# RWKV-7 mixer stage: two inverse streams interleaved at another distance, and other work moved around them

## The reference, cut to what matters

```python
hn = _rms_norm(h, e_norm_mix)
p = hn @ e_w_in                                   # 1024 -> 512 + 512 + 1792
pu, pv, pb = _split(p, [A_WIDTH, A_WIDTH, B_IN])
ya = _chunked_sgu(jax.nn.gelu(pu), jax.nn.gelu(pv), sgu_ln_g, sgu_ln_b, sgu_w, sgu_b)
yb = _rwkv7_time_mix(pb, ...)
h = h + jnp.concatenate([ya, yb], axis=-1) @ e_w_out
...
def _rwkv7_scan(r, w, k, v, kk, a):               # 8 heads of 64, one step a token
    def step(S, inp):
        r_t, w_t, k_t, v_t, kk_t, a_t = inp
        sa = jnp.einsum('bhij,bhj->bhi', S, kk_t)
        ...
```

## Time and profile before

| what | value |
|---|---|
| median of three runs | 1999.3 us (1998.69 to 2001.7) |
| the profiled execution's own time | 1999.16 us |
| its span | 1997.3 us |
| TensorE busy | 97% of the span |
| DVE / ACT / POOL busy | 76% / 58% / 19% |
| mean granted TensorE clock | 0.99 |
| the mixer's own part, last projection steps to second out tile | about 1095 to 1205 us of the span |

### The profile page before, as it was taken

How to read it: one execution, slowest core, us unless ns; L and a number is a source line. 1 busy time by engine, 2 the same in 40 slices (tenths; PEclk the granted TensorE clock), 3 DMA queues, 4 the chain that set the end, 5 groups by cost and what they waited for, 6 DMA issues and landing times.

```text
span 1997.3 us, 33816 instructions
## 1 busy us (share of the span) xinstructions
PE 1936.2 (97%) x12750; PEld 1699.1 (85%) x12750; DVE 1527.2 (76%) x2150; ACT 1148.8 (58%) x1709; POOL 371.5 (19%) x179
## 2 busy tenths in 40 slices
PE   7999998999999999999999899999999999999997
PEld 6888987988888889988879788888988788888885
DVE  6777876777777778777777866777786789888887
ACT  5444564644554464654455555444566677777775
POOL 2222021322222220122222222322003000000000
PEclk9999998999999999999999999999999999999999
DMA  9555441555555554355554105555562788888894
GB/s 353 191 189 189 154 142 64 180 190 189 191 187 191 189 169 159 127 192 190 190 166 158 65 33 179 191 189 190 182 228 85 283 319 320 320 321 329 328 334 185
DMA packets 73403, 401.08 MB, mean 201 GB/s; under 512 B 8256, under 2 KB 8384, under 8 KB 41152
## 3 DMA queue, kind: packets, MB, share of 16 engines
q1 hardware_dynamic: 72848, 397.81, 57.2%
q10 hardware_dynamic: 432, 1.57, 0.2%
HBM read 398.30 MB, written 1.05 MB: 200 GB/s over the span
## 4 chain that ended last, share of the span: by engine, by line
PE 83%; DVE 10%; PEld 4%; ACT 2%; issue 1%; DMA 0%; SPq 0%; ACTq 0%; DVEq 0%; PEldq 0%
PE psum L819 20%; PE psum L343 13%; PE psum L344 12%; PE psum L345 12%; PE psum L799 11%; DVE w_lo L311 2%; PE psum L576 2%; PE psum L588 2%; PE psum L3587 1%; PE psum L578 1%; PE psum L1184 1%; DVE w_lo L317 1%; PEld psum L345 1%; PEld psum L343 1%; PEld psum L344 1%
## 5 line engine op out<-in xcount | busy, mean ns | idle before, releaser
L311 DVE TENSOR_TENSOR w_lo<-ring,w_hi 128x1024 fp32r<-128x1024 f32 x498 | 739.5, 1514 | 176.4 <-ACT w_hi L304 175.1
L304 ACT ACTIVATE w_hi<-ring 128x1024 fp32r<-128x1024 f32 x744 | 739.8, 1051 | 210.9 <-PEq L537 110.8
L317 POOL TENSOR_TENSOR w_lo<-ring,w_hi 128x1024 fp32r<-128x1024 f32 x132 | 326.2, 2471 | 1093.5 <-ACT w_hi L304 1093.5
L819 PE MATMUL psum<-fT,w_hi 128*128 128x512 f32 x1760 | 421.7, 391 | 3.8 <-ACT w_hi L304 3.8
L819 PEld LDWEIGHTS psum<-fT,w_hi 128*128 128x128 f32 x1760 | 330.0, 188 | 72.0 <-ACT w_hi L304 4.2
L343 PE MATMUL psum<-w_hi,hT_hi 128*128 128x512 f32 (+3 forms) x656 | 241.8, 369 | 3.8 <-DVE hT_lo L1648 2.0
L343 PE MATMUL psum<-w_hi,act_hi 128*128 128x512 f32 x596 | 234.3, 393 | 0.8 <-DVE act_lo L3867 0.7
L799 PEld LDWEIGHTS psum<-fT,w_lo 128*128 128x128 f32 x1760 | 226.0, 191 | 8.9
L344 PE MATMUL psum<-w_lo,act_hi 128*128 128x512 f32 x596 | 233.3, 392 | 0.0
L345 PE MATMUL psum<-w_hi,hT_lo 128*128 128x512 f32 (+3 forms) x656 | 232.4, 354 | 0.0
L345 PE MATMUL psum<-w_hi,act_lo 128*128 128x512 f32 x596 | 232.1, 389 | 0.0
(11 more groups left out here) (579 smaller groups left out, 2529.1 us busy)
## 6 DMA issues: line engine op xcount, KB each, us to landing
ring<-in_stream SPq DMA_DIRECT2D x249, 1024.0 KB, 5.4
ring<-in_stream SPq DMA_DIRECT2D x248, 512.0 KB, 4.2
tables<-in_tables SPq DMA_DIRECT2D x1, 2005.0 KB, 19.3
gain_row<-in_gains ACTq DMA_DIRECT2D x3, 512.0 KB, 3.4
rows<-in_rows SPq DMA_DIRECT2D x1, 1288.0 KB, 22.0
X<-in_x SPq DMA_DIRECT2D x1, 1024.0 KB, 5.1
result<-X SPq DMA_DIRECT2D x2, 512.0 KB, 3.3
columns<-in_columns SPq DMA_DIRECT2D x1, 993.0 KB, 15.1
```

What stands on the lines that cost most here:

```text
L304: act.activation(part(w_hi, g, i), ring[:, k, i * PART:(i + 1) * PART], ACT.Copy) \
L311: dve.tensor_tensor(part(w_lo, g, i), ring[:, k, i * PART:(i + 1) * PART], part(w_hi, g, i).bitcast(F32), ALU.subtract) \
L317: pool.tensor_tensor(part(w_lo, g, 2), ring[:, k, 2 * PART:STEP], part(w_hi, g, 2).bitcast(F32), ALU.subtract) \
L819: pe.matmul(psum[:, 4 + 2 * (s % 2) + o, :], w[0][:, o, k, :], fT[:, k, :, :].rearrange("p a c -> p (a c)"), start=k == 0, stop=False, ski ...
```

## The change

On TensorE the order of the groups changes: stream a's levels come first, stream b follows three levels behind, and L, R and B of a half stand right before the places where their banks are needed; both `gating` groups stand after the inverses. `turn(1, 4)` moves behind the first half (k = 0 to 3) of the second out tile, which is now written by `out_part` in `second()` and `rest()`, and the seven unread matmuls go. ACT runs the gelu between the last projection tiles (`gelu_begun`, `gelu`), its statistics in pairs of groups, and some `split_hi` pieces earlier. POOL's levels follow the same order. DVE takes the reciprocal of the key norms before step 6's `split_lo` (`key_inverse`), the bonus products in two pairs, and `split_lo` pieces of the out-projection's first step earlier. The number of matmuls is the same apart from the seven; DVE, ACT and POOL do the same work (two of DVE's groups are split).

The diff, without ACT's, POOL's and half of DVE's lists of calls, which only stand in another order (the three fragments below it show DVE and TensorE):

```diff
@@ -671,11 +671,11 @@
                 for _, s, j in [x for x in tiles if x[0] == mine][-1:]:
                     eng.wait_ge(*after(f"used {name} {s} {j}"))
 
-        def out_tensor(pe, name, at, tiles=KT, after_first=None, warm=0, turns=2, begun={}):
+        def out_tensor(pe, name, at, tiles=KT, after_first=None, warm=0, turns=2, begun={}, first=None):
 
             g0, into_ffn = first_step[at] + STEPS[NETWORK[at][0]] - OUT_STEPS, NETWORK[at + 1][0] == "ffn"
             if into_ffn:
-                skip_banks(2 if begun else 0 if after_first is None else 8 - turns)
+                skip_banks(first if first is not None else 2 if begun else 0 if after_first is None else 8 - turns)
             heads = {(1, 0): lambda: head_tensor(pe, at + 1, (0,)), (2, 0): lambda: head_tensor(pe, at + 1, (1, 2))}
             routes = {(1, 0): lambda: route_turn_tensor(pe, at + 1, 0), (1, 1): lambda: router_tensor(pe, range(0, 2), True),
                       (2, 0): lambda: [route_turn_tensor(pe, at + 1, p) for p in (1, 2)]}
@@ -2806,63 +2806,82 @@
             values()
             gate(0)
             turn_products(pe, a)
-            gate(1)
+            level_products(pe, a, 1)
             matrix(1, "A")
-            level_products(pe, a, 1)
-            bonus()
             update_products(pe, a, 1)
             matrix(0, "L")
+            level_products(pe, a, 2)
+            gate(1)
+            update_products(pe, a, 2)
+            matrix(0, "R")
+            level_products(pe, a, 3)
             turn_products(pe, b)
-            level_products(pe, a, 2)
-            matrix(0, "R")
-            update_products(pe, a, 2)
+            update_products(pe, a, 3)
+            matrix(0, "B")
+            level_products(pe, a, 4)
             level_products(pe, b, 1)
-            level_products(pe, a, 3)
-            matrix(0, "B")
-            update_products(pe, a, 3)
-            level_products(pe, a, 4)
+            update_products(pe, a, 4)
+            key_rows()
             update_products(pe, b, 1)
-            key_rows()
-            update_products(pe, a, 4)
+            level_products(pe, a, 5)
             level_products(pe, b, 2)
+            update_products(pe, a, 5)
+            bonus()
+            update_products(pe, b, 2)
+            level_products(pe, a, 6)
+            level_products(pe, b, 3)
+            update_products(pe, a, 6)
             matrix(1, "L")
-            level_products(pe, a, 5)
-            update_products(pe, b, 2)
-            matrix(1, "R")
-            update_products(pe, a, 5)
-            level_products(pe, b, 3)
-            matrix(1, "B")
-            level_products(pe, a, 6)
             update_products(pe, b, 3)
             right_side(0, 0)
-            update_products(pe, a, 6)
             level_products(pe, b, 4)
             solved(0, 0)
             update_products(pe, b, 4)
+            matrix(1, "R")
             state(0)
             level_products(pe, b, 5)
             result(0, 0)
             update_products(pe, b, 5)
             right_side(0, 1)
-            gating(0, range(4))
+            matrix(1, "B")
             level_products(pe, b, 6)
             solved(0, 1)
             update_products(pe, b, 6)
             result(0, 1)
+            skip_banks(3)
             right_side(1, 0)
-            skip_banks(5)
+            gating(0, range(4))
+            solved(1, 0)
             gating(1, range(4))
-            solved(1, 0)
             state(1)
             result(1, 0)
             right_side(1, 1)
             turn(0, 0)
-            solved(1, 1, 1)
+            solved(1, 1)
             turn(1, 0)
             result(1, 1)
             turn(0, 4)
 
-            out_tensor(pe, "rwkv", at, after_first=lambda: turn(1, 4), turns=1, warm=6)
+            g = g0 + len(R_KINDS)
+            w = [x[:, g % 2, :].rearrange("p (k c) -> p k c", k=KT) for x in (w_hi, w_lo)]
+
+            def out_part(ks, first=False, last=False):
+                for k in ks:
+                    ins = three_passes(pe, bank("rwkv out 0 1")[:, 0:COLS], [x[:, k, P:SEQ] for x in (hT_hi, hT_lo)],
+                                       [x[:, k, 0:COLS] for x in w], first and k == ks[0], last and k == ks[-1])
+                return ins
+
+            def second():
+                open_bank(pe, "rwkv out 0 1")
+                pe.wait_ge(*after("rwkv hT 1 0"))
+                out_part(range(0, 4), first=True)
+                turn(1, 4)
+
+            def rest():
+                pe.wait_ge(*after("rwkv hT 1 4"))
+                return out_part(range(4, KT), last=True)
+
+            out_tensor(pe, "rwkv", at, after_first=second, turns=1, warm=0, begun={(0, 1): rest}, first=7)
 
         def rwkv_scalar(act, at):
             def does(label, *args, **kw):
...
@@ -2901,7 +2920,20 @@
                 act.wait_ge(*after("rwkv e2"))
                 does("rwkv exp", r_c[:, :, :], r_c[:, :, :], ACT.Exp, scale=NEG_ROOT_E)
 
-            proj_copies_scalar(act, "rwkv", at, R_KINDS, r_place, later={2: gates, 3: sigmoids, 4: key_root, 6: exps})
+            def gelu(gs):
+                for t in range(TT):
+                    for g in gs:
+                        x = r_tok[:, t, 512 + g * P:512 + (g + 1) * P]
+                        does("rwkv gelu", x, x, ACT.Gelu_apprx_tanh, accum_out=r_gsum[:, 0, 4 * t + g:4 * t + g + 1])
+
+            def gelu_begun():
+                wait_proj(act, "rwkv", R_KINDS, range(RWKV_T, RWKV_T + 2))
+                gelu((0, 1))
+                does("rwkv gelu u", r_tok[:, :, 0:512], r_tok[:, :, 0:512], ACT.Gelu_apprx_tanh)
+
+            proj_copies_scalar(act, "rwkv", at, R_KINDS, r_place, later={2: gates, 3: sigmoids, 4: key_root, 6: exps, 7: gelu_begun})
+            wait_proj(act, "rwkv", R_KINDS, range(RWKV_T, RWKV_T + RWKV_K))
+            gelu((2, 3))
             def values(t):
                 act.wait_ge(*after(f"rwkv v {t}"))
                 does(f"used rwkv v {t}", r_v[:, t, :], bank(f"rwkv v {t}"), ACT.Copy)
...
@@ -3176,6 +3201,10 @@
                 does("rwkv exponents", dve.tensor_tensor, r_ld[:, :, :], r_c[:, :, :], r_ld[:, :, :], ALU.subtract)
 
             key = r_pm[:, KEY:KEY + 4, :]
+
+            def key_inverse():
+                dve.wait_ge(*after("rwkv kn root"))
+                does("rwkv kn inverse", dve.reciprocal, r_kn[:, :], r_kn[:, :])
 
             def keys():
                 dve.wait_ge(*after("used rwkv a 1"))
@@ -3191,11 +3220,11 @@
                 settle()
                 does("rwkv b", dve.tensor_tensor, r_a[:, :, :], r_kk[:, :, :], r_a[:, :, :], ALU.mult)
 
-            def bonus():
-                for c in range(4):
+            def bonus(cs):
+                for c in cs:
                     does("rwkv rk", dve.scalar_tensor_tensor, r_rk[:, c, :], r_pm[:, REC + c, :], col("r_k")[:, c:c + 1], r_pm[:, KEY + c, :], ALU.mult, ALU.mult)
 
-            proj_copies_vector(dve, "rwkv", at, R_KINDS, r_place, lasts=R_LASTS,
+            proj_copies_vector(dve, "rwkv", at, R_KINDS, r_place, lasts=R_LASTS, between={4: key_inverse},
                                later={1: lambda: mix(0), 2: lambda: mix(1), 3: lambda: mix(2), 4: running_sums, 5: lambda: (exponents(), mix(3)),
                                       6: lambda: (mix(4), keys())})
             def decayed_keys(half):
@@ -3215,6 +3244,7 @@
 
             decayed_keys(0)
             decayed_keys(1)
+            bonus((0, 1))
 
             def bonus_sums():
                 dve.wait_ge(*after("rwkv bonus"))
...
             update_vector(dve, b, 6)
-            gating(0)
+            g = first_step[at] + len(R_KINDS)
+            split_lo(dve, g, g, (0,))
             result(0, 1)
             variances(1, 0)
             normalise(0, 0)
+            gating(0)
+            state(1)
             gating(1)
-            state(1)
             normalise(1, 0)
+            split_lo_last(dve, g, g)
             result(1, 0)
             variances(0, 1)
-            g = first_step[at] + len(R_KINDS)
-            split_lo(dve, g, g, (0,))
-            normalise(0, 1)
             split_lo(dve, g, g, (1,))
-            split_lo_last(dve, g, g)
             turn(0, 0)
             turn(1, 0)
+            normalise(0, 1)
             turn(0, 4)
             result(1, 1)
             variances(1, 1)
             split_lo(dve, g + 1, g + 1, (0,))
             normalise(1, 1)
             split_lo(dve, g + 1, g + 1, (1,))
+            turn(1, 4)
             split_lo_last(dve, g + 1, g + 1)
-            turn(1, 4)
             out_vector(dve, "rwkv", at, ahead=2)
 
 
```

118 lines of the change are left out of this document (56 added, 62 removed).

## The result

The changed kernel takes 2003.14 us (median of 20 runs, 1999.48 to 2006.42), the kernel before 2000.19 (20 runs): ratio 1.0014 [1.0008, 1.0020], 2.95 us slower. The forecast was 1997.2, and its range ended at 2000.5.

What follows compares the result with a forecast made beforehand. TensorE, busy 97% of the span, was taken as the bound, with about 17 us of waits and clock loss to win. Inverses 5.6 us earlier less 3.7 in the tail gave 1.9: 1999.16 to 1997.2 us, range 1992 to 2000.5.

Steps and rivals of the forecast that it cites:

- The early reciprocal: Head: DVE's key-norm reciprocal runs at about 1095.3, so `spread` starts about 1099.5 at full clock and matrix A at 1118.1.
- Gelu between the projection's tiles: Head: ACT's gelu, about 5 us, fits in ACT's idle 12.4 of 25 us and delays nothing.
- the 2.3 us: Head: matrix A starts at 1118.1 instead of 1120.38.
- The tail's loss: Outputs, behind the inverses: the tail gives back 3.7 us, the second tile's second half starting at R + 27.8, before R + 24.1.
- R: Start of the second half's right side, forecast 1173.3, before 1178.89; in "A to R", A is the start of matrix A.
- a plain wait of 3.2 us for O: Tail: TensorE ends its products at R + 14.0, waits until R + 17.2, then has a low clock for 3.9 us.
- the one on the inverses: Inverses: the stretch from matrix A takes 55.2 us, so its end, R, comes 5.6 us earlier.
- 1.5 of stops: Inverses: TensorE's waits for instruction packets add 1.5 us, as half of five stops would fall into waits already counted.
- A: Rival, chance 0.33: the tail's waits don't drop the clock and instruction stops are hidden, 1993.0 us.
- C: Rival, chance 0.08: dense inverses outrun instruction supply, a packet every 5.1 us, + 6.3 us, 2003.5 us.
- B: Rival, chance 0.14: DVE's tail doesn't shorten, two lock waits with POOL of 0.9 us each, 1999.0 us, no change.
- D: Rival, chance 0.02: nothing changes, `spread` starts no earlier because something else holds step 6.

Runs made afterwards that it cites:

- e3: Kernel before with only the first half of the second out tile ahead of the last turn, DVE's last split behind its turn: 1998.2 us, ratio 0.9994.
- e7: Changed kernel with the reciprocal late and the out-projection called as before, leaving the new orders: 2002.1 us, ratio 1.0014.
- e5: Changed kernel with 64 small matmuls added in TensorE's wait ahead of matrix A: 2000.5 us, ratio 1.0002.
- e1: Changed kernel with ACT's root of the first tile put back behind the copy of the last solution: 2002.3 us, ratio 1.0012.
- e4: Changed kernel with 128 empty instructions ahead of matrix A that never reached the program, so a repeat of it: 2002.3 us, ratio 1.0017.
- e10: e9 with the 64 small matmuls of e5 ahead of matrix A: 1998.6 us, ratio 0.9997.
- e12: Changed kernel with 96 small matmuls ahead of matrix A: 2000.7 us, ratio 1.0018.
- e13: Changed kernel with DVE normalising the first tile before a split and two turns' copies, ACT's order left as changed: 2000.5 us, ratio 1.0007.
- e15: e9 with DVE's split of the projection's last piece moved behind the copy of the first tile's last turn: 1998.7 us, ratio 0.9993.
- e2: Kernel before with only the reciprocal of the key norms moved ahead of step 6's split: 1999.3 us, ratio 0.9997.
- e6: Kernel before with the early reciprocal of e2 and the early second out tile of e3 together: 1997.2 us, ratio 0.9991.
- e11: e6 with the 64 small matmuls ahead of matrix A: 1996.9 us, ratio 0.9987.
- e14: e6 with DVE's tail in the changed kernel's order and ACT's root ahead of the last solution's copy: 2010.7 us, ratio 1.0059.
- e8: Changed kernel with e1's ACT order and six keep-warm matmuls back ahead of the output projection: 2002.1 us, ratio 1.0012.
- e9: Changed kernel with e1's ACT order and DVE normalising the first tile before a split and two turns' copies: 1997.5 us, ratio 0.9996.

## Why the prediction was wrong, point by point

**Right.** The early reciprocal: `spread` began at 1099.46 (forecast 1099.6), matrix A at 1118.18 after a wait of 2.59 us (forecast 1118.1, nearly 3). The 32 matmuls took 1.97 us, not half of 3.06; that fell into the wait. Gelu between the projection's tiles delayed nothing there: ACT is busy 17.7 of 23.2 us. But the 2.3 us were counted from one profile in which the clock had fallen behind the old wait; e3 and e7 show that it need not.

**Right in the number, by luck.** The tail's loss: the third turn at R + 17.2 (forecast 17.2), the second half of tile 2 at R + 28.1 (forecast 27.8), 4.0 us given back by the stage's end where I had 3.7. What I had put down as a plain wait of 3.2 us for O was in truth ACT's root ahead of the copy, 2.25 us, with DVE's order behind it. The clock was then low for 6.8 us instead of 3.9. The shorter wait and the longer stretch nearly cancel. (The 3.9 was a misreading besides: the row of 0.86 in the earlier trace rows puts the end of the stretch near 1106.3, so that it lasted 3.4 us.)

**The step that failed is the one on the inverses.** Forecast: 47.1 of work + 1.9 of clock + 4.7 of waits + 1.5 of stops = 55.2. Measured: 50.63 busy, so 3.5 of clock; 59.10 - 50.63 = 8.47 idle, of which 3.87 stops and 4.60 waits. The waits' sum was right, their places only in part: 2.67 us of it are two waits at the start of stream a, 1.27 for its first T and 1.40 for r_Y, that I had not named. The stops were 2.4 us larger, the clock 1.6, together 3.9 (4.0 by the starts), and R came at 1177.3 in place of 1173.3, past the 1176 that I had named as the mark of being wrong. I had argued that half of the stops would fall into waits already counted; instead there were fewer of them and two were of 1.7 us, a size that the trace of before does not have. The step left out is in the sizes: I took them from the order of before, where the work between two stops fills most of the 3.6 us at least that lie between them, and denser work leaves more of that time open (e5). The clock's loss came from elsewhere too: none behind the 2.59 us wait at matrix A, but 6.8 us at half rate behind the stop at 1149.

**How much of it holds beyond one profile.** The eleven kernels with the changed order of the inverses (after, e1, e4, e5, e7 to e10, e12, e13, e15) took 57.5 us from A to R in the mean, the five with the order of before that have no wait of their own there (before, e2, e3, e6, e11) 58.7. So the new order does gain, but 1.1 us, not 3.3, and the stops are most of what is missing: 3.6 us in the mean of those eleven against 2.4 in the five, and 1.5 in my sum.

**The sum.** -2.2 (head) + 0.6 (inverses) + 4.0 (tail) = +2.4 us in the stage of the profiled pair; the runs say +2.95. With the typical 57.5 us for the inverses it would be only -2.2 - 1.0 + 4.0 = +0.8. The two profiled executions differ by more than the stage, 4.7 us. The other 2.4 lie behind it, where nothing was edited: 790.35 us for 787.93, with the clock at its lower level for 14.4 us in place of 7.0. These stretches lie near 1551 and in the program's last 20 us, far from the stage, and they don't go with the change: e2 and e3 have 16.3 us of them, e6 6.8 and e15 7.0. Against the forecast of 1997.2 the profiled execution (2003.88) is 6.7 us late: 3.9 in the inverses, 0.3 in the tail, and 2.4 behind the stage, for which the forecast had no term. In the sixteen profiles other than e14's that rest took between 787.6 and 792.0 us, least where the clock was low for 7 us (before, e6, e15), most where it was for 19.5 (e1, e5).

e7, e1 and e8 have stages no longer than before by their profiles (115.1 to 115.7 us against 115.6) and still take 2.1 to 2.3 us more by their runs. The clock of all their runs, and not of the profiled one alone, can account for it in two of them: granted in the mean 0.9879 in e7 and 0.9885 in e1 against 0.9898 in the kernel before beside them, which is 3.8 and 2.6 us of clock in 2000 (e8: 0.9893, 1.0 us). The changed kernel had 0.9877, e9 0.9903, e6 and e11 0.9915 and 0.9913. In which part of the program the clock fell in those runs is not recorded.

**Where the sign came from.** I had entered the tail's 3.7 us as a fixed price of the early inverses. It was a price of two lists of calls, ACT's and DVE's: e9 takes 3 us of it back in the profile and 5.7 us in the median (4.8 against e4, the changed kernel's repeat; 3.6 by the ratios), by moving one call on ACT and two on DVE. With them the changed kernel is level with before (0.9996 [0.9987, 1.0004]); without the new orders, e6 and e11 are as fast or faster.

**The rivals.** A (the clock holds, the stops are hidden) had both wrong. C gave 2003.5 us and the sign. Its mechanism, dense work that outruns the supply of instructions, is what the stops show; its price is not. It had every block come after 5.1 us and 4.4 us from that. The stops ended 4 us apart (1137.33, 1141.27, 1145.31, 1149.28) in one dense part of the stretch and cost 2.4 us more than counted. The rest of what C had comes from elsewhere (the sum above), so that its 2003.5 is close by luck. In B, one of the two meetings of DVE and POOL did occur (the product with r_g at 1181.46 took 1.32 us, 0.42 before), but DVE had the state at R + 7.5 where the forecast had 7.4, and TensorE did not wait for it. D is out, as `spread` started 2.7 us earlier.

The Trainium skill (Runtime: NRT & Kernel Launch, Instruction fetch mechanics) has blocks of 256 instructions whose crossing is mostly hidden. The comb of 125 records, 250 instructions and a few more between them, agrees with the size; the 3.9 us of stops in the changed kernel don't agree with the hiding.
